# Attention with sinks: the sink as a 129th score column in PSUM, exponentials from PSUM, four probability buffers

## The chip, the cores and the metric

The kernel runs on one core of a Trainium2 chip. The metric is the device time of one execution in microseconds. Before the change three runs gave 2563.44 us (median), 2560.73 us and 2566.36 us.

## The reference

A trunk of two layers over 1024 tokens of width 1024. Each layer has a token mixer and a squared-ReLU MLP, both pre-normalised and modulated. Layer 0 mixes by sliding-window grouped-query attention, the part that the change touches. There are 16 heads of width 64 in two key-value groups of eight; a chunk of 64 queries sees 128 keys (its own chunk and the one before), and each head has a learned sink that takes part in the softmax but has no value:

```python
scores = jnp.einsum('bnqhgd,bnkhd->bnhgqk', q, kk).astype(jnp.float32) * (HEAD_DIM ** -0.5)
scores = jnp.where(valid[None, :, None, None, None, :], scores, -jnp.inf)
m = jnp.maximum(jnp.max(scores, axis=-1, keepdims=True), sink)
p = jnp.exp(scores - m)
probs = p / (jnp.sum(p, axis=-1, keepdims=True) + jnp.exp(sink - m))
o = jnp.einsum('bnhgqk,bnkhd->bnqhgd', probs.astype(vv.dtype), vv)
```

(The last line is the product of the probabilities with the values of the window.) Layer 1 mixes by a chunked gMLP. All is float32.

## The kernel before

Activations lie transposed, features on the partitions and 1024 tokens along the free dimension. The large products run as units of 128 output features: three products of high and low parts (L1034) into the PSUM tile pp[0] or pp[1], with weights loaded by SP, split by ScalarE (L298) and GpSimd (L267).

The attention stage lies between the QKV units and the units of the output projection. It has 32 steps t, two for each of the 16 chunks: t = 2n + g is chunk n and key-value group g. A step works on 4 pairs of heads, r = 0 to 3, each a block of 128 query rows (two heads by 64 queries) by 128 keys. What happens to step t:

- SP loads the queries (`load_q`, L243) into qf[g].
- TensorE `scores` (L1185): four products into one bank of pp[0] (bank g). It waits until the bank is free (p_sub of t - 2) and for the load.
- VectorE `maxima` (L870 to L879): row maxima of the scores, the maximum with 8 times the sink (L872), the sink's column minus the maximum (L877), and the scores minus the maximum from PSUM into the SBUF tile pr[g] (L879). Every small operation waits for the one before by a semaphore.
- ScalarE `exps` (L465): one exponential over 516 columns of pr[g] in place. `window` (L470), every second step, copies the values of the chunk's window.
- VectorE `sums` (L859, L861): row sums and their reciprocals.
- GpSimd `normalise` (L279): pr[g] times the reciprocals.
- TensorE `turn` (L1194): four transposes of pr[g] into a bank of pp[1].
- ScalarE `probs_copy` (L454): that bank into the SBUF tile pt[g].
- TensorE `mix` (L1202): one product with the window's values into a bank of pp[2]; 128 rows are computed, and only the 64 rows of group g are used.
- ScalarE `out_high` (L459) and VectorE `out_low` (L887): the 64 rows by 512 columns as high and low part, once a step.

No planner orders this. Each engine has its own hand-written loop over t, with the steps staggered, and executes it strictly in its order. TensorE in step t does scores(t+1), mix(t-2), turn(t-1). ScalarE does probs_copy(t-2), out_high(t-3), exps(t) and, in even steps, window. VectorE does sums(t-1), maxima(t), out_low(t-3). Four steps make one pass of a hardware loop. After the last step TensorE waits for all `out_low` before the output projection begins (L1034 again), and ScalarE then issues the 8 MB load of mod_late.

Of the kernel before, what the change touches and what calls it, by code (L numbers as in the profile page):

```python
# [48 lines left out]
def build(nc, x_in, c_in, pos_in, weights, mod_w, cols, mats, ws_in, bias_in, q_dram, v_dram, out):  # L49
# [5 lines left out]
    with ctx:  # L55
# [21 lines left out]
        sink8 = sb("sink8", [P, 2 * 4])  # L77
# [8 lines left out]
        with ExitStack() as attn:  # L86
            kf = sb("kf", [HD, KV, PAD + S], f32, attn)
            vt = sb("vt", [P, PAD + S], f32, attn)
            v_s = sb("v_s", [P, NCH, P], f32, attn)
            with ExitStack() as rope:  # L90
                cos = sb("cos", [P, S], f32, rope)
                sin = sb("sin", [P, S], f32, rope)
                qa = sb("qa", [P, 2, S], f32, rope)
                qb = sb("qb", [P, 2, S], f32, rope)
                oa = sb("oa", [P, 2, S], f32, rope)
                ob = sb("ob", [P, 2, S], f32, rope)
            qf = sb("qf", [HD, 2, HALF], f32, attn)
            pr = sb("pr", [P, 2, 4, P + 1], f32, attn)
            pt = sb("pt", [P, 2, HALF], f32, attn)
            v_w = sb("v_w", [P, 2, P], f32, attn)  # L100
            small = sb("small", [P, 2, 4, 4], f32, attn)
# [25 lines left out]
        qgain_a, qgain_b, kgain = (colt[:, o + i:o + i + 1] for i in range(3))  # L127
# [35 lines left out]
        sc_mm, p_sub, p_exp, p_sum, p_norm = sem("sc_mm"), sem("p_sub"), sem("p_exp"), sem("p_sum"), sem("p_norm")  # L163
        p_tr, p_cp, vw, pv_mm, o_hi, o_lo = (sem(n) for n in ("p_tr", "p_cp", "vw", "pv_mm", "o_hi", "o_lo"))
        p_tot, p_max = sem("p_tot"), sem("p_max")
# [9 lines left out]
        sink8_done = sem("sink8_done")  # L175
# [19 lines left out]
        def columns_of(half):  # L195
            return slice(HALF * half, HALF * half + HALF)

# [66 lines left out]
        def _(pool):  # L264
# [12 lines left out]
            def normalise(t, g):  # L277
                pool.wait_ge(p_sum, t + 1)  # L278
                nc.gpsimd.tensor_tensor(out=pr[:, g, :, 0:P], in0=pr[:, g, :, 0:P],  # L279
                                        in1=small[:, g, 3, :].unsqueeze(2).to_broadcast([P, 4, P]),  # L280
                                        op=ALU.mult).then_inc(p_norm, 1)

            with pool.Fori(0, NCH) as n:  # L283
                for g in range(KV):
                    normalise(n * 2 + g, g)
# [7 lines left out]
        def _(act):  # L293
# [156 lines left out]
            def probs_copy(t, g):  # L450
# [3 lines left out]
                nc.scalar.activation(pt[:, g, :], pp[1][:, HALF * g:HALF * g + HALF], ACT.Copy).then_inc(p_cp, 1)  # L454

            def out_high(t, n, g):
                act.wait_ge(pv_mm, t + 1)
                rows = slice(64 * g, 64 * g + 64)
                nc.scalar.activation(h_hi[rows, :, bass.ds(n * CHUNK, CHUNK)],  # L459
                                     pp[2][rows, HALF * g:HALF * g + HALF].rearrange("p (h t) -> p h t", t=CHUNK),  # L460
                                     ACT.Copy).then_inc(o_hi, 1)

            def exps(t, g):
                act.wait_ge(p_sub, t + 1)
                nc.scalar.activation(pr[:, g, :, :], pr[:, g, :, :], ACT.Exp, scale=HD ** -0.5).then_inc(p_exp, 1)  # L465

            def window(t, n, e):
                if not static(t) or t >= 4:
                    act.wait_ge(pv_mm, t - 2)
                nc.scalar.activation(v_w[:, e, :], v_s[:, bass.ds(n, 1), :].rearrange("p a c -> p (a c)"),  # L470
                                     ACT.Copy).then_inc(vw, 1)
# [12 lines left out]

            act.wait_ge(v_cp, 4)
            for b in range(4):
                step(0, b)
            with act.Fori(1, NCH // 2 - 1) as m:
                for b in range(4):
                    step(m, b)  # L490
            for b in range(7):
                step(NCH // 2 - 1 + b // 4, b % 4)
# [11 lines left out]
            act.wait_ge(o_lo, 2 * NCH)  # L504
# [104 lines left out]
        def _(dve):  # L609
# [148 lines left out]
            V.tensor_scalar(sink8[:, :], colt[:, sink0:sink0 + 2 * 4], 8.0, None, ALU.mult).then_inc(sink8_done, 1)  # L758
# [96 lines left out]
            def sums(t, g):  # L855
                dve.wait_ge(p_exp, t + 1)
                if not static(t) or t >= 2:
                    dve.wait_ge(p_norm, t - 1)
                V.tensor_reduce(out=small[:, g, 2, :], in_=pr[:, g, :, :], axis=X, op=ALU.add).then_inc(p_tot, 1)  # L859
                dve.wait_ge(p_tot, t + 1)  # L860
                V.reciprocal(small[:, g, 3, :], small[:, g, 2, :]).then_inc(p_sum, 1)  # L861

            def maxima(t, g):

                lo = PAD if static(t) and t < 2 else 0
                sc = pp[0][:, HALF * g:HALF * g + HALF].rearrange("p (r k) -> p r k", k=P)
                dve.wait_ge(sc_mm, t + 1)
                if not static(t) or t >= 2:
                    dve.wait_ge(p_tr, t - 1)
                V.tensor_reduce(out=small[:, g, 0, :], in_=sc[:, :, lo:], axis=X, op=ALU.max).then_inc(p_max, 1)  # L870
                dve.wait_ge(p_max, t * 2 + 1)
                V.tensor_tensor(out=small[:, g, 1, :], in0=small[:, g, 0, :], in1=sink8[:, 4 * g:4 * g + 4],  # L872
                                op=ALU.max).then_inc(p_max, 1)
                dve.wait_ge(p_max, t * 2 + 2)
                if lo:
                    V.memset(pr[:, g, :, 0:lo], -1.0e4)
                V.tensor_tensor(out=pr[:, g, :, P:P + 1], in0=sink8[:, 4 * g:4 * g + 4].unsqueeze(2),  # L877
                                in1=small[:, g, 1, :].unsqueeze(2), op=ALU.subtract)
                V.tensor_tensor(out=pr[:, g, :, lo:P], in0=sc[:, :, lo:],  # L879
                                in1=small[:, g, 1, :].unsqueeze(2).to_broadcast([P, 4, P - lo]),  # L880
                                op=ALU.subtract).then_inc(p_sub, 1)

            def out_low(t, n, g):
                rows = slice(64 * g, 64 * g + 64)
                cs = bass.ds(n * CHUNK, CHUNK)
                dve.wait_ge(o_hi, t + 1)
                V.tensor_tensor(out=h_lo[rows, :, cs],  # L887
                                in0=pp[2][rows, HALF * g:HALF * g + HALF].rearrange("p (h t) -> p h t", t=CHUNK),
                                in1=h_hi[rows, :, cs].bitcast(f32), op=ALU.subtract).then_inc(o_lo, 1)

            def step(m, b):
                t = m * 4 + b
                if not static(t) or 1 <= t < 2 * NCH + 1:
                    sums(t - 1, (b + 1) % 2)
                if not static(t) or t < 2 * NCH:
                    maxima(t, b % 2)
                if not static(t) or 3 <= t:
                    out_low(t - 3, m * 2 + ((b + 1) // 2 - 2), (b + 1) % 2)

            dve.wait_ge(sink8_done, 1)  # L900
            for b in range(4):
                step(0, b)
            with dve.Fori(1, NCH // 2 - 1) as m:
                for b in range(4):
                    step(m, b)
            for b in range(7):
                step(NCH // 2 - 1 + b // 4, b % 4)
# [112 lines left out]
        def _(pe):  # L1020
# [159 lines left out]
            def scores(t, n, g):  # L1180
                pe.wait_ge(qf_in[g], n * 16 + 16)
                if not static(t) or t >= 2:
                    pe.wait_ge(p_sub, t - 1)
                for r in range(4):
                    last = T.matmul(pp[0][:, HALF * g + P * r:HALF * g + P * r + P], qf[:, g, P * r:P * r + P],  # L1185
# [3 lines left out]
            def turn(t, g):  # L1189
                pe.wait_ge(p_norm, t + 1)  # L1190
                if not static(t) or t >= 2:
                    pe.wait_ge(p_cp, t - 1)
                for r in range(4):
                    last = T.transpose(pp[1][:, HALF * g + P * r:HALF * g + P * r + P], pr[:, g, r, 0:P], ident[:, :])  # L1194
                last.then_inc(p_tr, 1)

            def mix(t, n, g, e):
                pe.wait_ge(p_cp, t + 1)
                pe.wait_ge(vw, n + 1)
                if not static(t) or t >= 2:  # L1200
                    pe.wait_ge(o_lo, t - 1)
                T.matmul(pp[2][:, HALF * g:HALF * g + HALF], v_w[:, e, :], pt[:, g, :],  # L1202
                         start=True, stop=True).then_inc(pv_mm, 1)
# [11 lines left out]
            pe.wait_ge(evac[0], U_WO // 2)  # L1215
# [3 lines left out]
            for b in range(4):  # L1219
                step(0, b)  # L1220
            with pe.Fori(1, NCH // 2 - 1) as m:
                for b in range(4):
                    step(m, b)
            for b in range(6):
                step(NCH // 2 - 1 + b // 4, b % 4)


            pe.wait_ge(o_lo, 2 * NCH)
# [167 lines left out]
```

## Time and profile before

| | us |
|---|---|
| median of the runs | 2563.44 |
| span of the profiled execution | 2568.1 |
| attention stage, first scores to first product of the output projection | 234.07 to 358.36 |

The profiled execution is 4.7 us above the median of the runs. Rows of groups give line, engine, operation, output and inputs with their shapes, the count, the busy time and the mean of one, and the idle time of the engine just before with the engine and line that ended it. Rows in order of time begin with the start and the duration in us; "x8" merges eight instructions, and the bracket holds the idle time before and who ended it. A matmul's end is modelled, so that its duration holds a drain that overlaps with the next; the distance between two starts is what it costs in a queue that doesn't wait. PEclk 1.00 is a granted clock of 2.4 GHz and 0.50 one of 1.2 GHz.

### The profile page before, as it was taken

The numbers are of one execution on the slowest core, as the hardware profiler recorded it, in microseconds if no ns is written. First come the engines' busy times: TensorE is split into PE (matmuls) and PEld (weight loads), VectorE is DVE, ScalarE is ACT, GpSimd is POOL, SyncE is SP. The second block draws the span as 40 slices with busy tenths as digits, with TensorE's granted clock in tenths as the row PEclk, the third lists the DMA queues.
The fourth block names the chain that finished last, engine by engine and source line by source line (L and its number), as shares of the span: only waits on it lengthen the run. The fifth ranks groups of instructions, "written<-read, shape, count | busy, mean of one in ns | idle before, by whom it ended". The sixth has DMA issues, their size and how long they took to land.

```text
span 2568.1 us, 28722 instructions
## 1 busy us (share of the span) xinstructions
PE 2438.0 (95%) x10592; PEld 1942.8 (76%) x10592; DVE 1059.8 (41%) x1190; ACT 650.8 (25%) x719; POOL 506.9 (20%) x232
## 2 busy tenths in 40 slices
PE   3997889899999999998999999999899999999999
PEld 2776458688888888887788788788678888888887
DVE  7655965633333333334432442343522323232232
ACT  3322531321221221212322331122331221221221
POOL 1111221112212212211211112112122221222121
PEclk9887989899999999999999999999899999999999
DMA  6342131121221221221244221221011111111112
GB/s 240 107 140 68 37 150 41 64 84 49 75 80 49 83 72 52 87 66 41 98 127 143 89 74 41 73 82 49 25 49 50 49 41 50 49 47 43 49 49 82
DMA packets 70592, 189.01 MB, mean 74 GB/s; under 512 B 23440, under 2 KB 25360, under 8 KB 70032
## 3 DMA queue, kind: packets, MB, share of 16 engines
q1 hardware_dynamic: 52144, 127.64, 15.4%
q10 hardware_dynamic: 18400, 60.69, 6.8%
q8 instruction: 35, 0.57, 0.1%
q14 instruction: 13, 0.11, 0.0%
HBM read 170.48 MB, written 16.78 MB: 73 GB/s over the span
## 4 chain that ended last, share of the span: by engine, by line
issue 65%; PE 27%; POOL 7%; POOLq 0%; DVE 0%; ACT 0%; DVEq 0%
PE pp L1034 27%; POOL w_lo L267 7%; POOL pr L279 1%; POOLq L287 0%; POOLq L266 0%; DVE x L921 0%; POOLq L283 0%; DVE mod_t L624 0%; ACT tmp L307 0%; POOLq L273 0%; POOLq L278 0%; POOL kf L270 0%; POOLq L267 0%; POOL vt L271 0%; DVEq L921 0%
## 5 line engine op out<-in xcount | busy, mean ns | idle before, releaser
L267 POOL TENSOR_TENSOR w_lo<-w_raw,w_hi 128x1024 fp32r<-128x1024 f32 x194 | 473.2, 2439 | 1942.4 <-ACT w_hi L298 1942.4
L1034 PE MATMUL pp<-h_hi,w_hi 128*128 128x512 f32 x1824 | 605.7, 408 | 35.1 <-DVE h_lo L715 23.3
L1034 PE MATMUL pp<-h_lo,w_hi 128*128 128x512 f32 x1824 | 595.2, 402 | 0.0
L1034 PE MATMUL pp<-h_hi,w_lo 128*128 128x512 f32 x1824 | 593.7, 401 | 0.0
L298 ACT ACTIVATE w_hi<-w_raw 128x1024 fp32r<-128x1024 f32 x194 | 205.0, 1057 | 959.6 <-PE pp L1034 916.9
L1034 PEld LDWEIGHTS pp<-h_hi,w_hi 128*128 128x128 f32 x1824 | 346.6, 192 | 129.3 <-issue 22.4
L1034 PEld LDWEIGHTS pp<-h_lo,w_hi 128*128 128x128 f32 x1824 | 350.5, 192 | 85.3 <-issue 1.0
L1034 PEld LDWEIGHTS pp<-h_hi,w_lo 128*128 128x128 f32 x1824 | 349.6, 192 | 85.7
L1034 PE MATMUL pp<-hid_hi,w_hi 128*128 128x512 f32 x1280 | 410.4, 398 | 0.0
L1034 PE MATMUL pp<-hid_hi,w_lo 128*128 128x512 f32 x1280 | 409.0, 397 | 0.0
L1034 PE MATMUL pp<-hid_lo,w_hi 128*128 128x512 f32 x1280 | 408.9, 397 | 0.0
L921 DVE SCALAR_TENSOR_TENSOR x<-pp,mod,x 128x1024 f32 (+1 forms) x82 | 104.8, 1278 | 481.1 <-PE pp L1034 481.0
L1034 PEld LDWEIGHTS pp<-hid_lo,w_hi 128*128 128x128 f32 x1280 | 241.2, 188 | 59.0 <-issue 0.5
L1034 PEld LDWEIGHTS pp<-hid_hi,w_lo 128*128 128x128 f32 x1280 | 241.2, 188 | 58.7
L1034 PEld LDWEIGHTS pp<-hid_hi,w_hi 128*128 128x128 f32 x1280 | 240.7, 188 | 58.4 <-issue 0.5
L944 DVE SCALAR_TENSOR_TENSOR tmp<-pp,tmp 128x1024 f32<-128x1024 f32 x64 | 78.3, 1224 | 335.2 <-ACT tmp L525 335.2
L624 DVE TENSOR_TENSOR mod_t<-mod_t,tmp 128x1024 f32<-128x1024 f32 x90 | 169.9, 1888 | 105.4 <-ACT tmp L307 104.6
L525 ACT ACTIVATE tmp<-pp 128x1024 f32<-128x1024 f32 x64 | 65.7, 1026 | 472.3 <-PE pp L1034 472.3
L947 DVE TENSOR_TENSOR hid_lo<-tmp,hid_hi 128x1024 f32 x64 | 119.2, 1863 | 87.0 <-ACT hid_hi L528 87.0
L627 DVE SCALAR_TENSOR_TENSOR mod_acc<-mod_t,cond,mod_acc 128x1024 f32<-128x1024 f32 x64 | 95.8, 1497 | 56.2 <-DMA mod_t<-mod_w 55.3
L307 ACT ACTIVATE tmp<-x 128x1024 f32 (+1 forms) x90 | 95.4, 1061 | 81.2 <-DVE x L921 72.8
L974 DVE BATCH_NORM_STATS2 v_stat<-pp 128x128 f32 x128 | 26.9, 282 | 122.6 <-PE pp L1280 122.6
(133 smaller groups left out, 1225.0 us busy)
## 6 DMA issues: line engine op xcount, KB each, us to landing
w_raw<-weights SPq DMA_DIRECT2D x194, 512.0 KB, 3.3
mod_t<-mod_w ACTq DMA_DIRECT2D x64, 512.0 KB, 3.4
mod_first<-mod_w SPq DMA_DIRECT2D x16, 512.0 KB, 15.5
mod_late<-mod_w ACTq DMA_DIRECT2D x2, 4096.0 KB, 19.3
v_dram<-v_out ACTq DMA_DIRECT2D x16, 512.0 KB, 5.5
vf<-v_dram ACTq DMA_DIRECT2D x16, 512.0 KB, 4.4
x<-x_in SPq DMA_DIRECT2D x4, 1024.0 KB, 9.1
qf<-q_dram SPq DMA_DIRECT2D x32, 128.0 KB, 2.5
```

What stands on the lines that cost most here:

```text
L267: nc.gpsimd.tensor_tensor(out=w_lo[:, s, :, :], in0=w_raw[:, s, :, :], in1=w_hi[:, s, :, :].bitcast(f32), op=ALU.subtract).then_inc(lo_don ...
L279: nc.gpsimd.tensor_tensor(out=pr[:, g, :, 0:P], in0=pr[:, g, :, 0:P], in1=small[:, g, 3, :].unsqueeze(2).to_broadcast([P, 4, P]), op=ALU.m ...
L298: nc.scalar.activation(w_hi[:, s, :, :], w_raw[:, s, :, :], ACT.Copy).then_inc(hi_done, 1)
L307: nc.scalar.activation(tmp[:, s, :], x[:, bass.ds(k, 1), :].rearrange("p a s -> p (a s)"), ACT.Square).then_inc(sq_done, 1)
L525: nc.scalar.activation(tmp[:, s, :], pp[s][:, :], ACT.Relu).then_inc(relu, 1)
L624: V.tensor_tensor(out=sumsq, in0=sumsq, in1=tmp[:, s, :], op=ALU.add).then_inc(ss_done, 1)
L627: V.scalar_tensor_tensor(out=mod_acc[:, :], in0=tile, scalar=cond[:, 2, bass.ds(k, 1)], in1=mod_acc[:, :], op0=ALU.mult, op1=ALU.add).then ...
L921: V.scalar_tensor_tensor(out=xn, in0=pp[s][:, :], scalar=mod[:, gate, bass.ds(i * 2 + s, 1)], in1=xn, op0=ALU.mult, op1=ALU.add).then_inc( ...
L944: V.scalar_tensor_tensor(out=tmp[:, s, :], in0=pp[s][:, :], scalar=0.0, in1=tmp[:, s, :], op0=ALU.max, op1=ALU.mult).then_inc(evac[s], 1)
L947: V.tensor_tensor(out=hid_lo[:, bass.ds(i * 2 + s, 1), :].rearrange("p a s -> p (a s)"), in0=tmp[:, s, :], in1=hid_hi[:, bass.ds(i * 2 + s ...
L974: ins = V.bn_stats(v_stat[:, b, bass.ds(c, 1), :].rearrange("p a s -> p (a s)"), pp[2][:, P * b:P * b + P])
L1034: last = T.matmul(pp[s][:, cs], w[:, s, k, :], r[:, k, cs], start=(k == 0 and w is w_hi and r is hi), stop=(k == KC - 1 and w is w_lo))
```

## The change

The attention step is rebuilt:

- The query gain is multiplied by 64 ** -0.5 once (`qgain`), so that scores need no scale, and the sinks are used as they are.
- A score tile is now a whole pp tile (pp[0] for g = 0, pp[3] for g = 1), two banks with 2 x 129 columns each. The sinks are written as column 128 of every block once before the stage and stay there.
- `maxima` is one reduction over 129 columns in PSUM with its result negated. `exps` is four exponentials of 129 columns each that read PSUM, take the negated maximum as bias, and write pr. The maximum with the sink and both subtractions are gone.
- pr and small have four buffers, and `turn` works two steps behind instead of one.
- The two groups' values lie in v_w with zeros between them, so that two `mix` products (g = 0 starts, g = 1 adds) fill all 128 rows of one bank. `out_high` and `out_low` run once per chunk over 128 rows. v_w is zeroed once.
- `probs_copy` is on VectorE for g = 0 and on ScalarE for g = 1.
- The order within a step changes on all three engines: TensorE mix(t-3), scores(t+1), turn(t-2); ScalarE exps(t), window (even t), probs_copy(t-2) (odd t), out_high (even t); VectorE maxima(t), sums(t-1), probs_copy(t-2) (even t), out_low (odd t).
- Scores wait for the exponentials of t - 2 (p_exp), where they waited for the subtraction.

```diff
+        def score_tile(g):
+            return (pp[0], pp[3])[g][:, :].rearrange("p (a c) -> p a c", a=2)[:, :, 0:2 * (P + 1)].rearrange(
+                "p a (b k) -> p a b k", b=2)
...
+            def exps(t, b):
+                lo = PAD if static(t) and t < 2 else 0
+                sc = score_tile(b % 2)
+                act.wait_ge(p_max, t + 1)
+                if not static(t) or t >= 4:
+                    act.wait_ge(p_tr, t - 3)
+                for r in range(4):
+                    ins = nc.scalar.activation(pr[:, b, r, lo:], sc[:, r // 2, r % 2, lo:], ACT.Exp,
+                                               bias=small[:, b, 0, r:r + 1])
+                ins.then_inc(p_exp, 1)
...
             def step(m, b):
                 t = m * 4 + b
-                if not static(t) or 2 <= t < 2 * NCH + 2:
-                    probs_copy(t - 2, b % 2)
-                if not static(t) or 3 <= t:
-                    out_high(t - 3, m * 2 + ((b + 1) // 2 - 2), (b + 1) % 2)
                 if not static(t) or t < 2 * NCH:
-                    exps(t, b % 2)
+                    exps(t, b % 4)
                     if b % 2 == 0:
-                        window(t, m * 2 + b // 2, b // 2)
+                        window(m * 2 + b // 2, (b // 2) % 2)
+                if b % 2 and (not static(t) or 3 <= t < 2 * NCH + 2):
+                    probs_copy(t - 2, m * 2 + ((b - 1) // 2 - 1))
+                if b % 2 == 0 and (not static(t) or t >= 4):
+                    out_high(m * 2 + (b // 2 - 2), (b // 2) % 2)
...
+            def maxima(t, b):
+                lo = PAD if static(t) and t < 2 else 0
+                sc = score_tile(b % 2)
+                dve.wait_ge(sc_mm, t + 1)
+                if lo:
+                    V.memset(pr[:, b, :, 0:lo], 0.0)
+                V.tensor_reduce(out=small[:, b, 0, :].rearrange("p (a b) -> p a b", a=2), in_=sc[:, :, :, lo:], axis=X,
+                                op=ALU.max, negate=True).then_inc(p_max, 1)
+            def probs_copy(t, n):
+                dve.wait_ge(p_tr, t + 1)
                 if not static(t) or t >= 2:
+                    dve.wait_ge(pv_mm, t - 1)
+                V.tensor_copy(pt[:, 0, :], pp[1][:, 0:HALF]).then_inc(p_cp[0], 1)
...
             def step(m, b):
                 t = m * 4 + b
+                if not static(t) or t < 2 * NCH:
+                    maxima(t, b % 4)
                 if not static(t) or 1 <= t < 2 * NCH + 1:
-                    sums(t - 1, (b + 1) % 2)
+                    sums(t - 1, (b + 3) % 4)
+                if b % 2 == 0 and (not static(t) or 2 <= t < 2 * NCH + 2):
+                    probs_copy(t - 2, m * 2 + (b // 2 - 1))
+                if b % 2 and (not static(t) or t >= 5):
+                    out_low(m * 2 + ((b - 1) // 2 - 2), ((b - 1) // 2) % 2)
...
             def step(m, b):
                 t = m * 4 + b
+                if not static(t) or 3 <= t < 2 * NCH + 3:
+                    mix(m * 2 + ((b + 1) // 2 - 2), (b + 1) % 2, ((b + 1) // 2) % 2)
                 if not static(t) or t + 1 < 2 * NCH:
                     scores(t + 1, m * 2 + (b + 1) // 2, (b + 1) % 2)
                 if not static(t) or 2 <= t < 2 * NCH + 2:
-                    mix(t - 2, m * 2 + (b // 2 - 1), b % 2, (b // 2 + 1) % 2)
-                if not static(t) or 1 <= t < 2 * NCH + 1:
-                    turn(t - 1, (b + 1) % 2)
+                    turn(t - 2, m * 2 + (b // 2 - 1), (b + 2) % 4)
```

## Rows read from the trace of the kernel before

**Rows 1.** The page: span, and busy time by engine (share of the span, instructions).
```profile
span 2568.1 us, 28722 instructions
...
PE 2438.0 (95%) x10592; PEld 1942.8 (76%) x10592; DVE 1059.8 (41%) x1190; ACT 650.8 (25%) x719; POOL 506.9 (20%) x232
```

**Rows 2.** Busy time by stretch: bounds, length, then PE, PEld, DVE, ACT, POOL (instructions), PEclk, DMA share, GB/s.
```profile
247.30:305.30 58.00, 47.89 (x235) 28.26 (x235) 54.23 (x115) 30.09 (x58) 16.86 (x17) 1.00 0.13 36
305.30:308.70 3.40, 3.40 (x12) 2.19 (x11) 3.09 (x8) 1.72 (x3) 0.82 (x2) 0.50 0.15 39
...
349.60:363.30 13.70, 10.12 (x22) 5.74 (x21) 4.72 (x8) 3.37 (x6) 1.04 (x1) 0.50 0.30 95
```

**Rows 3.** Groups of instructions, VectorE alone, 253 to 336 us.
```profile
L879 DVE TENSOR_TENSOR pr<-pp,small 128x512 f32<-128x512 f32 x24 | 16.4, 684 | 0.0
L887 DVE TENSOR_TENSOR h_lo<-pp,h_hi 64x512 f32 x24 | 16.4, 683 | 0.4
L870 DVE TENSOR_REDUCE small<-pp 128x4 f32<-128x512 f32 x23 | 15.9, 691 | 0.4
L859 DVE TENSOR_REDUCE small<-pr 128x4 f32<-128x516 f32 x23 | 15.9, 691 | 2.0 <-ACT pr L465 1.0
L872 DVE TENSOR_TENSOR small<-small,sink 128x4 f32<-128x4 f32 x23 | 9.1, 396 | 0.8
L861 DVE RECIPROCAL small<-small 128x4 f32<-128x4 f32 x23 | 4.1, 178 | 0.8
L877 DVE TENSOR_TENSOR pr<-sink,small 128x4 f32<-128x4 f32 x23 | 3.8, 167 | 0.8
```

**Rows 4.** Who waited for whom, 250 to 345 us: total us, times, longest us.
```profile
ACT pr L465 <- DVE pr L879: 46.3, 27, 1.9
...
PE pp L1185 <- DVE pr L879: 5.6, 24, 0.3
```

**Rows 5.** Groups of instructions, ScalarE and GpSimd, 236 to 358 us.
```profile
L279 POOL TENSOR_TENSOR pr<-pr,small 128x512 f32<-128x512 f32 x32 | 33.3, 1039 | 94.9 <-DVE small L861 94.9
...
L465 ACT ACTIVATE pr<-pr 128x516 f32<-128x516 f32 x32 | 20.3, 633 | 54.8 <-DVE pr L879 54.8
L454 ACT ACTIVATE pt<-pp 128x512 f32<-128x512 f32 x32 | 18.8, 588 | 3.5 <-PE pp L1194 3.1
...
L470 ACT ACTIVATE v_w<-v_s 128x128 f32 (+1 forms) x16 | 4.7, 293 | 0.0
```

**Rows 6.** TensorE in order of time, first steps of the stage.
```profile
239.09 2.07 PE L1185 MATMUL pp<-kf,qf 64*128 64x128 f32 x8 [1.24 <-DMA qf<-q_dram]
...
244.79 2.07 PE L1202 MATMUL pp<-pt,v_w 128*128 128x512 f32 x2
...
248.57 1.13 PE L1202 MATMUL pp<-pt,v_w 128*128 128x512 f32 x2
249.53 0.60 PE L1194 MATMUL pp<-ident,pr 128*128 128x128 f32 x4
250.06 1.16 PE L1185 MATMUL pp<-kf,qf 64*128 x8
251.15 1.12 PE L1202 MATMUL pp<-pt,v_w 128*128 128x512 f32 x2
...
253.29 1.15 PE L1185 MATMUL pp<-kf,qf 64*128 x8 [0.18 <-DVE pr L879]
```

**Rows 7.** TensorE in order of time, last scores to the output projection.
```profile
342.90 1.13 PE L1185 MATMUL pp<-kf,qf 64*128 64x128 f32 x8 [0.25 <-DVE pr L879]
...
352.95 1.06 PE L1194 MATMUL pp<-ident,pr 128*128 128x128 f32 x4
...
354.70 2.07 PE L1202 MATMUL pp<-pt,v_w 128*128 128x512 f32 x2 [0.69 <-ACT pt L454]
...
358.36 1.19 PE L1034 MATMUL pp<-h_hi,w_hi 128*128 128x512 f32 x2 [1.59 <-DVE h_lo L887]
```

More of the change, by code:

```diff
@@ L76, in build @@
         inv = sb("inv", [P, 4 * KC])
-        sink8 = sb("sink8", [P, 2 * 4])
+        qgain = sb("qgain", [P, 2])
         with ExitStack() as first:
@@ L126, in build @@
         o = 4 * KC + PARTS * KC
-        qgain_a, qgain_b, kgain = (colt[:, o + i:o + i + 1] for i in range(3))
+        kgain = colt[:, o + 2:o + 3]
+        qgain_a, qgain_b = qgain[:, 0:1], qgain[:, 1:2]
         inv_freq = colt[:, o + 3:o + 4]
@@ L275, in _, with normalise @@
                     split_lo(pair, s)
-            def normalise(t, g):
+            def normalise(t, b):
                 pool.wait_ge(p_sum, t + 1)
-                nc.gpsimd.tensor_tensor(out=pr[:, g, :, 0:P], in0=pr[:, g, :, 0:P],
-                                        in1=small[:, g, 3, :].unsqueeze(2).to_broadcast([P, 4, P]),
+                nc.gpsimd.tensor_tensor(out=pr[:, b, :, 0:P], in0=pr[:, b, :, 0:P],
+                                        in1=small[:, b, 3, :].unsqueeze(2).to_broadcast([P, 4, P]),
                                         op=ALU.mult).then_inc(p_norm, 1)
-            with pool.Fori(0, NCH) as n:
-                for g in range(KV):
-                    normalise(n * 2 + g, g)
+            with pool.Fori(0, NCH // 2) as m:
+                for b in range(4):
+                    normalise(m * 4 + b, b)
             with pool.Fori(U_WO // 2 + 1, UNITS // 2) as pair:
@@ L453, in probs_copy, with out_high, window @@
                     act.wait_ge(pv_mm, t - 1)
[L454 to L460, printed above, removed]
-                                     ACT.Copy).then_inc(o_hi, 1)
[L463 to L470, printed above, removed]
+                nc.scalar.activation(pt[:, 1, :], pp[1][:, HALF:], ACT.Copy).then_inc(p_cp[1], 1)
+            def out_high(n, e):
+                act.wait_ge(pv_mm, n * 2 + 2)
+                nc.scalar.activation(h_hi[:, :, bass.ds(n * CHUNK, CHUNK)],
+                                     pp[2][:, HALF * e:HALF * e + HALF].rearrange("p (h t) -> p h t", t=CHUNK),
+                                     ACT.Copy).then_inc(o_hi, 1)
+            def window(n, e):
+                if not static(n) or n >= 2:
+                    act.wait_ge(pv_mm, n * 2 - 2)
+                nc.scalar.activation(v_w[:, e, :].rearrange("p (g c) -> p g c", g=2)[:, :, 0:HD],
+                                     v_s[:, bass.ds(n, 1), :].rearrange("p a (g c) -> p (a g) c", g=KV),
                                      ACT.Copy).then_inc(vw, 1)
@@ L475, in step @@
                 t = m * 4 + b
[L476 to L479 removed]
                 if not static(t) or t < 2 * NCH:
[L481 removed]
+                    exps(t, b % 4)
                     if b % 2 == 0:
[L483 to L488 removed]
+                        window(m * 2 + b // 2, (b // 2) % 2)
[3 more added lines that the diff above has]
+                    out_high(m * 2 + (b // 2 - 2), (b // 2) % 2)
+            act.wait_ge(v_cp, 4)
+            act.wait_ge(vw_zero, 1)
+            for m in range(2):
+                for b in range(4):
+                    step(m, b)
+            with act.Fori(2, NCH // 2 - 1) as m:
                 for b in range(4):
@@ L491, in _ @@
             for b in range(7):
-                step(NCH // 2 - 1 + b // 4, b % 4)
+                step(NCH // 2 - 1, b)
             def residual(pair0, first=0, count=4, split=True):
@@ L757, in _ @@
             dve.wait_ge(const_in, 48)
-            V.tensor_scalar(sink8[:, :], colt[:, sink0:sink0 + 2 * 4], 8.0, None, ALU.mult).then_inc(sink8_done, 1)
+            own(V.tensor_scalar(qgain[:, :], colt[:, o:o + 2], HD ** -0.5, None, ALU.mult))
             dve.wait_ge(pos_s, 16)
@@ L852, in _, with sums @@
             mod_part(3)
-            def sums(t, g):
+            def sums(t, b):
                 dve.wait_ge(p_exp, t + 1)
-                if not static(t) or t >= 2:
[L858 to L881, printed above, removed]
@@ L883, in out_low @@
-            def out_low(t, n, g):
-                rows = slice(64 * g, 64 * g + 64)
+                if not static(t) or t >= 4:
+                    dve.wait_ge(p_norm, t - 3)
+                V.tensor_reduce(out=small[:, b, 2, :], in_=pr[:, b, :, :], axis=X, op=ALU.add).then_inc(p_tot, 1)
+                dve.wait_ge(p_tot, t + 1)
+                V.reciprocal(small[:, b, 3, :], small[:, b, 2, :]).then_inc(p_sum, 1)
+            def maxima(t, b):
[6 more added lines that the diff above has]
+                                op=ALU.max, negate=True).then_inc(p_max, 1)
@@ L885, in out_low, with probs_copy @@
+            def probs_copy(t, n):
+                dve.wait_ge(p_tr, t + 1)
+                if not static(t) or t >= 2:
+                    dve.wait_ge(pv_mm, t - 1)
+                V.tensor_copy(pt[:, 0, :], pp[1][:, 0:HALF]).then_inc(p_cp[0], 1)
+            def out_low(n, e):
                 cs = bass.ds(n * CHUNK, CHUNK)
[L886 to L889, printed above, removed]
+                dve.wait_ge(o_hi, n + 1)
+                V.tensor_tensor(out=h_lo[:, :, cs],
+                                in0=pp[2][:, HALF * e:HALF * e + HALF].rearrange("p (h t) -> p h t", t=CHUNK),
+                                in1=h_hi[:, :, cs].bitcast(f32), op=ALU.subtract).then_inc(o_lo, 1)
@@ L901, in _ @@
-            for b in range(4):
-                step(0, b)
-            with dve.Fori(1, NCH // 2 - 1) as m:
+                    sums(t - 1, (b + 3) % 4)
[3 more added lines that the diff above has]
+                    out_low(m * 2 + ((b - 1) // 2 - 2), ((b - 1) // 2) % 2)
+            dve.wait_ge(evac[0], U_WO // 2)
+            dve.wait_ge(v_cp, 4)
@@ L904, in _ @@
+            for g in range(KV):
+                V.tensor_copy(score_tile(g)[:, :, :, P:P + 1],
+                              colt[:, sink0 + 4 * g:sink0 + 4 * g + 4].rearrange("p (a b k) -> p a b k", a=2, b=2)).then_inc(sinks_in, 1)
+            dve.wait_ge(sinks_in, 2)
+            dve.wait_ge(q_out, 16 * 8 * 4)
+            dve.wait_ge(kf_in, 16 * 4)
+            V.memset(v_w[:, :, :], 0.0).then_inc(vw_zero, 1)
+            for m in range(2):
                 for b in range(4):
                     step(m, b)
-            for b in range(7):
-                step(NCH // 2 - 1 + b // 4, b % 4)
+            with dve.Fori(2, NCH // 2 - 1) as m:
+                for b in range(4):
+                    step(m, b)
@@ L910, in residual @@
+            for b in range(8):
+                step(NCH // 2 - 1, b)
             def residual(pair0, n0, gate, first=0, count=4, late=None, zeroed=None):
@@ L1218, in _ @@
             scores(0, 0, 0)
-            for b in range(4):
-                step(0, b)
-            with pe.Fori(1, NCH // 2 - 1) as m:
+            for m in range(2):
                 for b in range(4):
                     step(m, b)
-            for b in range(6):
-                step(NCH // 2 - 1 + b // 4, b % 4)
-            pe.wait_ge(o_lo, 2 * NCH)
+            with pe.Fori(2, NCH // 2 - 1) as m:
+                for b in range(4):
+                    step(m, b)
+            for b in range(7):
+                step(NCH // 2 - 1, b)
+            pe.wait_ge(o_lo, NCH)
             for late in range(2):
```

53 lines of the change are left out of this document (25 added, 28 removed).

## The prediction

> **What bounds the kernel now.** I read the page's busy times first: TensorE is busy for 95% of the span and VectorE for 41% [rows 1]. That average says nothing of the attention stage, so I went on to the windows. In the first 58 us of full clock in that stage VectorE is busy for 54.23 of 58.00 us, TensorE for 47.89, ScalarE for 30.09 and GpSimd for 16.86 [rows 2]. One step takes 3.584 us: the scores of step 6 start at 253.29 [rows 6] and those of step 31 at 342.90 [rows 7], 89.61 us for 25 steps. The groups of VectorE add up to 0.684 + 0.683 + 0.691 + 0.691 + 0.396 + 0.178 + 0.167 = 3.490 us a step [rows 3], with almost no idle time. So VectorE sets the pace, and the waits say the same: ScalarE's exponential waited for the subtraction in each of 27 steps, and TensorE's scores in 24 [rows 4]. TensorE follows closely. Where it ran from a queue that didn't wait (248.57 to 251.15), mix took 0.96 us from start to start, turn 0.53 and scores 1.09, or 2.58 us in all [rows 6].
>
> **What VectorE loses.** Per pair of steps the new code has two maxima and two sums (4 x 0.691), two reciprocals (2 x 0.178), one out_low (0.684; it covers 128 rows, with the same 512 columns) and one copy out of PSUM. No row shows such a copy on VectorE: ScalarE's takes 0.588 [rows 5], and VectorE's operations of that width out of PSUM take 0.684 to 0.691 [rows 3]. I take 0.691, the same engine. The pair comes to 4.495 us, or 2.25 us a step instead of 3.49. If VectorE or the queued TensorE (2.58) still set the pace, the stage would shrink by about 1.0 us a step.
>
> **What the new order makes of TensorE.** This step decides. Before, the order was turn(t-1), then scores(t+2), then mix(t-1): the copy of the transposed probabilities ran under the scores. Now a step is mix(t-3), scores(t+1), turn(t-2), and the next begins with mix(t-2), which waits for the copy of exactly what turn(t-2) has just written. Nothing of TensorE's lies between. Step by step:
> - mix start to scores start: 0.96 (mix to turn) [rows 6];
> - scores start to turn start: 1.09 (scores to mix) [rows 6];
> - turn from start to end: 0.60 [rows 6];
> - end of turn, semaphore, copy on ScalarE, semaphore, start of mix: 0.69, seen whole in the tail, where nothing else was in the way [rows 7].
>
> This makes 3.34 us for an odd step, whose copy is on ScalarE. An even step has VectorE's copy, 0.10 us longer (0.691 against 0.588), so 3.44. The mean is 3.39 us. TensorE is then a serial chain with one hole of about 0.7 us per step, and VectorE idles a third of the time.
>
> The copier must be free when turn ends, 2.65 us into the step. VectorE: after an odd step's out_low it takes maxima (when the scores end, some 2.2 us into the step), and sums, and reaches the copy about 0.4 us into the even step: free. Maxima(t+1) is queued behind the copy and so starts at 3.4 us; the exponential of that odd step starts 0.7 us into it, and ScalarE has until 2.65 for it, a slack of 1.95 us. Price of the four exponentials: a 128-column activation takes 0.293, so 4 x 0.293 = 1.17; were the fixed part free, it would be the 0.633 of 516 columns [rows 5]. I take 1.17 (the row with the same width): it fits either way and costs nothing. If that cover is gone, every microsecond above 1.95 is paid in every second step.
>
> The Trainium skill speaks against this edit: ScalarE: Activation LUTs, "Rules for kernel authors", budgets about 0.3 us for each activation plus 0.83 ns an element, four times over 1.63 us. By that page the step would still fit, with 0.3 us of slack instead of 0.8; the trace's 0.293 us for 128 columns is less than the rule's 0.41.
>
> The rest hides. Normalise stays at 1.039 us on GpSimd [rows 5] and, with four buffers, has a step more before its turn needs it. The scores' wait for exponentials of t - 2 is met over a step earlier. Out_high falls to once in two steps; ScalarE's load for a pair is 2 x 1.17 + 0.588 + 0.588 + 0.293 = 3.8 of 6.8 us. SP's query loads keep their place. Zeroing v_w (768 columns, at most 1.0 us by the rate of 512 columns in 0.691) and writing the sinks are queued ahead of the first maxima, while the first key load and scores are under way; the qgain operation replaces sink8 early.
>
> **The sum.** Against the profiled execution (span 2568.1):
> - Start. The third scores now wait for the first exponentials and begin at about 239.3 (239.09 before). Then at low clock two scores (2.07 each, as before), turn (1.06), copy (0.69), mix (2.07), and from the clock's rise scores 1.09, turn 0.60, copy 0.69: mix(1) at 249.6 [rows 6, 7]. Scores of step 6 follow mix(2): 249.6 + 3.39 + 0.96 = 254.0, where 253.29 stood: +0.7.
> - 25 steps at 3.39 instead of 3.584: -4.85.
> - Tail. From the last scores to the projection it took 358.36 - 342.90 = 15.46 us [rows 7]. Now, from those scores: turn(28) ends at 1.69, mix(28) at 2.48; without scores the following steps are mix 0.96, turn 0.60, copy 0.69 or 0.79, so mix(29) at 4.73, mix(30) at 7.08, mix(31) at 9.33; the mix itself takes 1.12 and the two output copies took 1.59 (358.36 less 354.70 + 2.07): 12.04 us, a gain of 3.42. The last exponentials and their normalising end near 6.7, before turn(31) at 8.04. That is at full clock. Before, the clock fell to 1.2 GHz at 349.6 and stayed there for 13.7 us [rows 2], and if it does so again from mix(30), two mixes and a turn lengthen by 0.95 + 0.46 + 0.95 = 2.4 and the gain is 1.1.
>
> Sum: 0.7 - 4.85 - 3.42 = -7.6 with a warm tail, 0.7 - 4.85 - 1.1 = -5.2 with a cold one. Should the projection also start warm, half of the 4.9 us from 358.36 to 363.3 comes on top: -10.1. TensorE pauses in the tail as often as before but more briefly, so I take the middle of the first two, -6.4. The later stages depend on nothing in this one except its end: the mod_late load and the projection start together, as before. The median of the runs is 4.7 us below the profiled execution's span, and I move it by the same amount: 2563.4 - 6.4 = 2557.0.
>
> **The rivals.**
> - Exponentials from PSUM slower than thought, or copies caught behind other work on ScalarE or VectorE. Each 0.4 us more on the hole costs 0.4 x 29 = 12 us. An exponential stage of 2.2 us (0.55 each) would add 0.25 in every second step, +4: 2561. For it: four instructions with a bias operand from PSUM, which no row shows. Against it: 0.8 us of slack. The page named above would sharpen it without reaching it. Chance 0.10, mostly "same".
> - The slower side: the granted clock. The hole is now one piece of 0.7 us every step, and the clock already dropped once in mid-stage, at 305.30, for 3.4 us, though TensorE was busy around it [rows 2]. Before, low clock in mid-stage was covered, since VectorE set the pace. Now every TensorE term lies in the chain: a low step costs 2.07 + 2.07 + 1.06 + 0.7 = 5.9 less overlaps of some 0.2, 5.7 instead of 3.39, or +2.3. It decides from 5 low steps on (6.4 + 5.1 = 11.5 us, 28 us of low clock). If it stayed low for 20 of the 31, 2557.0 + 46 = 2603. Against it: TensorE's work in a step is the same as before and the step is shorter, so its share of work rises from 2.58 / 3.584 to 2.58 / 3.39. Chance 0.09.
> - The serial chain doesn't hold, because the rows' modelled ends overstate it: if the chain is only the queued 2.58 plus 0.4, 3.0 us a step, this gives 29 x 0.4 = 12 us more: 2545. The wait for the copy is in the program's order, so I give it 0.06.
> - The chain as summed: 0.75.
>
> **How the numbers follow.** A measurement of this kernel can tell about 0.2%, 5.1 us, from no change. The forecast's own cases run from -3 (start worse, cold tail) to -10, and the cold tail stands right at that bound: of its 0.75 I put 0.54 beyond and 0.21 within. The first rival gives 0.08 to same and 0.02 to slower, the clock 0.09 to slower, the last 0.06 to faster. Faster 0.60, same 0.29, slower 0.11. The range reaches from 2550 (warm throughout, with part of the last rival) to 2565 (copies late by 0.25 in every step, +7).
>
> **What would show it.** In the profile after: step period 3.3 to 3.5 us; TensorE's mix waits about 0.7 us in nearly every step for the copy, half of the time on ScalarE and half on VectorE; VectorE idles about 1.1 us a step, most of it before its copy, ended by the transposes; four exponentials take 0.8 to 1.2 us together; the projection starts 5 to 8 us earlier. It is wrong if mix waits much longer than 0.8 us, if the scores wait for exponentials, or if PEclk shows 0.50 in the stage for more than one short piece.

## The result, and the profile after

The changed kernel takes 2631.36 us (median of 4 runs, 2627.88 to 2635.11) against 2564.67 us for the kernel before (median of 4, a run of 2565.90 us having joined the three of the first section): a ratio of 1.0261 with a 95% interval of 1.0244 to 1.0277. It is slower by 67 us where 6 us less were forecast.

The page of the changed kernel comes first: span, busy times, and TensorE's granted clock in 40 slices.

```profile
span 2627.4 us, 28569 instructions
...
PE 2494.2 (95%) x10592; PEld 1973.4 (75%) x10592; DVE 1023.1 (39%) x1097; ACT 649.9 (25%) x783; POOL 506.5 (19%) x232
...
PEclk8996557999999999999899999999899999999999
```

VectorE has lost 37 us of work against [rows 1], as intended. TensorE has 56 us more, with the same number of products: they have become slower. PEclk shows where, in the slices from about 200 to 420 us. The window of the stage (columns as in [rows 2]):

```profile
240.00:400.00 160.00, 139.38 (x380) 81.08 (x380) 56.97 (x110) 49.35 (x152) 29.15 (x28) 0.50 0.08 21
```

The granted clock is 0.50, or 1.2 GHz, for the whole 160 us; the kernel before had 1.00 over most of the stage [rows 2]. TensorE in order of time shows how the stage begins, a step, and how it ends:

```profile
228.96 3.78 PE L1210 MATMUL pp<-kf,qf 64*128 64x128 f32 x16 [3.17 <-DMA kf<-oa]
...
253.48 2.07 PE L1210 MATMUL pp<-kf,qf 64*128 64x128 f32 x8
...
257.29 2.07 PE L1229 MATMUL pp<-pt,v_w 128*128 128x512 f32 x2 [0.69 <-ACT pt L474]
259.29 2.07 PE L1210 MATMUL pp<-kf,qf 64*128 64x128 f32 x8
261.30 1.11 PE L1220 MATMUL pp<-ident,pr 128*128 128x128 f32 x4
263.19 2.08 PE L1229 MATMUL pp<-pt,v_w 128*128 128x512 f32 x2 [0.78 <-DVE pt L896]
...
400.64 2.07 PE L1210 MATMUL pp<-kf,qf 64*128 64x128 f32 x8
...
415.49 2.07 PE L1229 MATMUL pp<-pt,v_w 128*128 128x512 f32 x2 [0.69 <-ACT pt L474]
419.15 1.19 PE L1059 MATMUL pp<-h_hi,w_hi 128*128 128x512 f32 x2 [1.59 <-DVE h_lo L901]
```

Mix (L1229), scores (L1210), turn (L1220), then a hole of 0.69 us where ScalarE copies and 0.78 us where VectorE does. That is the serial chain of the forecast, with each term at the low clock: 2.00 + 2.01 + 1.11 + 0.78 = 5.90 us for the step from 257.29 to 263.19, and 5.81 us where the hole is 0.69. From the scores of step 6 (253.48) to those of step 31 (400.64) it is 147.16 us for 25 steps, 5.89 us each instead of 3.584. From 240 to 400 us the engine waits for nothing else:

```profile
PE pp L1229 <- DVE pt L896: 11.8, 14, 0.9
PE pp L1229 <- ACT pt L474: 9.6, 14, 0.7
```

The first scores stood at 228.96 and the projection began at 419.15: 190.2 us for the stage, where the table gave 124.3. These 66 us are the result; what follows the stage takes 2208.3 us (2627.4 less 419.15) against 2209.7. What precedes it took 5.1 us less than in the profile of the kernel before (228.96 against 234.07), but this part scatters: in the profiles of the experiments below whose code is the same up to there, the first scores stand anywhere from 228.99 to 236.20. The length of the stage is therefore the better measure of one profile against another.

### The profile page after: what moved, and what is told of

The parts are those of the page before. It is cut to its first block, busy times and chain, and to the rows that moved or that the text cites. A ratio compares the mean times of both kernels' runs of the same rounds, so it can differ in the third digit from the quotient of the medians.

```text
span 2627.4 us, 28569 instructions
## 1 busy us (share of the span) xinstructions
PE 2494.2 (95%) x10592; PEld 1973.4 (75%) x10592; DVE 1023.1 (39%) x1097; ACT 649.9 (25%) x783; POOL 506.5 (19%) x232
## 4 chain that ended last, share of the span: by engine, by line
issue 65%; PE 27%; POOL 8%; POOLq 0%; DVE 0%; ACT 0%; DVEq 0%
PE pp L1059 27%; POOL w_lo L274 7%; POOL pr L286 1%; POOLq L294 0%; POOLq L273 0%; DVE x L946 0%; DVE mod_t L642 0%; ACT tmp L314 0%; POOLq L285 0%; POOLq L290 0%; POOLq L280 0%; POOL kf L277 0%; POOLq L274 0%; POOL vt L278 0%; DVEq L946 0%
## 5 line engine op out<-in xcount | busy, mean ns | idle before, releaser
L1210 PEld LDWEIGHTS pp<-kf,qf 64*128 64x128 f32 x256 | 56.8, 325 | 47.0 <-issue 42.1
```

Source lines behind the costliest of these rows:

```text
L1210: last = T.matmul(score_tile(g)[:, r // 2, r % 2, 0:P], qf[:, g, P * r:P * r + P], kf[:, g, bass.ds(n * CHUNK, P)], start=True, stop=True)
```

## The experiments

Two theories were set against each other. By the first, the new order of TensorE's step makes a hole in each step, and with it a clock that starts low never rises. By the second, something else of the change (the score tiles of two banks, exponentials from PSUM, too little work in a step) slows the stage, and the order doesn't matter.

### Scores ahead of mix again

```diff
             def step(m, b):
                 t = m * 4 + b
-                if not static(t) or 3 <= t < 2 * NCH + 3:
-                    mix(...)
                 if not static(t) or t + 1 < 2 * NCH:
                     scores(...)
+                if not static(t) or 3 <= t < 2 * NCH + 3:
+                    mix(...)
```

> The changed kernel with one edit: in TensorE's step scores(t+1) stands before mix(t-3) again, so that it covers the copy between turn and mix. Theory 1 (the order makes a hole in every step, and the granted clock stays at 1.2 GHz as long as it is there): no hole, the clock rises to 2.4 GHz within the first steps, a step takes 2.6 to 2.8 us instead of 5.86, the stage shrinks from about 189 us to about 100, total 2530 to 2545 us. Theory 2 (the clock stays low because each step has too little work for TensorE, whatever the order): a clock of 1.2 GHz throughout, steps of about 5.1 us (2.00 + 2.00 + 1.1), total about 2607 us.

Measured: 2538.98 us (2535.81 to 2541.32), ratio to the kernel before 0.991 (0.9888 to 0.9932). Swapping two calls is worth 92 us against the changed kernel. TensorE in order of time, and the window of the loop:

```profile
248.64 1.21 PE L1210 MATMUL pp<-kf,qf 64*128 64x128 f32 x8
249.79 1.12 PE L1229 MATMUL pp<-pt,v_w 128*128 128x512 f32 x2
250.75 0.60 PE L1220 MATMUL pp<-ident,pr 128*128 128x128 f32 x4
251.37 1.13 PE L1210 MATMUL pp<-kf,qf 64*128 64x128 f32 x8
...
316.05 1.13 PE L1210 MATMUL pp<-kf,qf 64*128 64x128 f32 x8
```
```profile
253.00:315.00 62.00, 60.00 (x324) 40.56 (x323) 46.72 (x91) 41.41 (x125) 23.82 (x23) 1.00 0.16 49
```

The hole ahead of mix is gone, the clock is 1.00, and TensorE is busy for 60 of 62 us. From the scores of step 6 (248.64) to those of step 31 (316.05) it is 67.41 us for 25 steps, 2.70 us each. So the new arithmetic does what it is for; VectorE, busy for 46.72 of 62 us, no longer sets the pace.

### The hole in the kernel before

The converse, with none of the new arithmetic:

```diff
             def step(m, b):
                 t = m * 4 + b
+                if not static(t) or 2 <= t < 2 * NCH + 2:
+                    mix(t - 2, ...)
                 if not static(t) or t + 1 < 2 * NCH:
                     scores(t + 1, ...)
-                if not static(t) or 2 <= t < 2 * NCH + 2:
-                    mix(t - 2, ...)
                 if not static(t) or 1 <= t < 2 * NCH + 1:
                     turn(t - 1, (b + 1) % 2)
```

> The kernel before with one edit: mix(t-2) stands ahead of scores(t+1) in TensorE's step, so that it follows turn(t-2) directly. Nothing of the new arithmetic. Theory 1: the same hole, the clock stays low through the stage, steps of about 5.8 us instead of 3.58, total 2620 to 2640 us. Theory 2 (something else of the change, such as the score tiles of two banks or exponentials from PSUM, holds TensorE down): the clock is high as before, VectorE sets the pace, total 2560 to 2575 us.

Measured: 2629.4 us, ratio 1.0261 (1.0234 to 1.0289), the very ratio of the whole change. A step takes 5.86 us. A window of its stage, and some of its steps:

```profile
260.00:400.00 140.00, 122.56 (x336) 71.47 (x335) 74.46 (x168) 44.08 (x84) 24.93 (x24) 0.50 0.07 22
```
```profile
247.83 2.07 PE L1202 MATMUL pp<-pt,v_w 128*128 128x512 f32 x2 [0.69 <-ACT pt L454]
249.83 2.07 PE L1185 MATMUL pp<-kf,qf 64*128 64x128 f32 x8
251.84 1.11 PE L1194 MATMUL pp<-ident,pr 128*128 128x128 f32 x4
253.90 2.07 PE L1202 MATMUL pp<-pt,v_w 128*128 128x512 f32 x2 [0.95 <-ACT pt L454]
```

The second theory falls with these two runs: the order alone makes the loss, and taking the order away removes the loss.

### Filling the hole with work that nobody needs

```diff
+            def fill(g, count):
+                for i in range(count):
+                    T.matmul(pp[1][:, HALF * (1 - g):HALF * (1 - g) + P], ident[:, :], ident[:, :], start=True, stop=True)
...
                     turn(t - 2, m * 2 + (b // 2 - 1), (b + 2) % 4)
+                    fill(b % 2, 2)
```

> The changed kernel, order untouched, with two extra 128x128x128 float32 products after each turn, into the bank of pp[1] that is free then; nothing reads them. They fill TensorE's hole with work that helps nobody. Theory 1 (the hole holds the clock down): the clock rises, a step takes 3.4 to 3.6 us, total 2555 to 2570 us although TensorE does more. Theory 2 (the order or the copies are slow for another reason, and the clock only follows): steps of 5.9 us as before the edit or more, total 2630 to 2640 us.

Measured: 2562.88 us (2557.54 to 2565.47), ratio 0.9996 (0.9985 to 1.0007). With the order of the changed kernel, and more work for TensorE, 68 us come back. In the profile the clock rose at about 253 us, and a step then took 3.57 us, as it does with open holes at high clock (the run with the filled start below). It is the clock, then, that makes the hole dear, not the hole's own 0.7 us.

> As filled (the changed kernel with extra products after each turn), but with one product instead of two, so that at low clock about 0.43 us of the 0.7 to 0.78 us hole are filled and 0.3 remain in every step. If any pause in every step holds the clock down: steps of 5.86 us, total 2625 to 2635 us. If it depends on the pause's share: the clock rises, steps of 3.5 us, total 2560 to 2568 us. I hold the second for likelier, since the kernel before rose from low clock with small pauses between its groups.

This one has `fill(b % 2, 1)`. Measured: 2565.54 us (2561.08 to 2572.82), ratio 1.0006 (0.9992 to 1.002). At low clock 0.36 us of hole were left ahead of the first mix, and the next group already ran fast:

```profile
244.05 0.63 PE L1234 MATMUL pp<-ident 128*128 128x128 f32 x2
245.04 2.08 PE L1229 MATMUL pp<-pt,v_w 128*128 128x512 f32 x2 [0.36 <-DVE pt L896]
247.05 1.16 PE L1210 MATMUL pp<-kf,qf 64*128 64x128 f32 x8
```

The time is that of the second branch, and one pause of 0.36 us didn't keep the clock from rising. The first branch isn't excluded by it: only that one short pause stood at low clock, the ones after it (0.46 to 0.72 us) came at high clock, so a short pause in every step at low clock remains untested.

### Filling at the start only

The same edit under `if static(t) and t < 8`: the extra products stand in the eight unrolled steps, and the loop is that of the changed kernel.

> As filled, but the extra products stand only in the first eight steps, which are unrolled; the loop over the other steps is that of the changed kernel. Theory 1a (low clock holds itself: once it is high, the steps of 3.4 us with 0.7 us of hole keep it high, since TensorE's share of work is larger than in the kernel before): clock 2.4 GHz to the tail, total about 2560 us. Theory 1b (the hole also pulls a high clock down): the clock falls again after the filled steps, steps of 5.86 us, total 2610 to 2630 us.

Measured: 2561.94 us (2557.96 to 2566.85), ratio 0.9996 (0.9984 to 1.0008). In the loop, long after the last extra product:

```profile
271.42 1.12 PE L1229 MATMUL pp<-pt,v_w 128*128 128x512 f32 x2 [0.94 <-DVE pt L896]
272.47 1.16 PE L1210 MATMUL pp<-kf,qf 64*128 x8
273.56 0.66 PE L1220 MATMUL pp<-ident,pr 128*128 128x128 f32 x4
274.91 1.13 PE L1229 MATMUL pp<-pt,v_w 128*128 128x512 f32 x2 [0.69 <-ACT pt L474]
...
278.49 1.12 PE L1229 MATMUL pp<-pt,v_w 128*128 128x512 f32 x2 [0.78 <-DVE pt L896]
...
285.71 1.12 PE L1229 MATMUL pp<-pt,v_w 128*128 128x512 f32 x2 [0.95 <-DVE pt L896]
...
347.26 1.16 PE L1210 MATMUL pp<-kf,qf 64*128 64x128 f32 x8
...
359.37 0.70 PE L1059 MATMUL pp<-h_hi,w_hi 128*128 128x512 f32 x2 [1.59 <-DVE h_lo L901]
```
```profile
270.00:333.00 63.00, 48.96 (x244) 29.13 (x243) 37.88 (x72) 31.42 (x97) 18.26 (x18) 1.00 0.12 38
```

The same instructions in the same order, with the same holes, keep a clock of 1.00 for the whole loop (and here to the end of the stage). The four steps from 271.42 to 285.71 take 14.29 us, 3.57 us each. The loop has two states, and the start chooses. Theory 1a holds and 1b falls.

> The kernel before with mix ahead of scores, and two extra products after each turn in its first eight steps only, as in filled_start. None of the new arithmetic. Theory 1a (two states of the same loop: low clock and a chain of 5.8 us, or high clock; what the start gives, stays): the clock is high after the start, and a step takes the longer of VectorE's 3.5 us and the chain's 3.4, so 3.5 to 3.6: total 2562 to 2572 us. Theory 1b (this loop falls back to low clock because VectorE's work adds pauses): 2610 to 2630 us.

This is the same test on the kernel before with its hole (eight steps unrolled on TensorE). Measured: 2565.24 us (2561.14 to 2570.07), ratio 1.0007 (0.9993 to 1.0021), against 2629.4 us without the filled start. Its window:

```profile
260.00:345.00 85.00, 66.58 (x339) 40.61 (x340) 79.64 (x168) 44.50 (x84) 23.94 (x24) 1.00 0.12 34
```

Again two states of one loop, at a clock of 0.50 or of 1.00. From the scores of step 8 to those of step 31 a step took 3.73 us, a little more than the 3.5 to 3.6 expected.

### A burst ahead of the stage

```diff
+            pe.wait_ge(evac[1], U_WO // 2)
+            fill(0, 7)
             pe.wait_ge(kf_in, 16 * 4)
             pe.wait_ge(sinks_in, 2)
-            pe.wait_ge(evac[1], U_WO // 2)
             pe.wait_ge(q_cs, 8)
             scores(0, 0, 0)
```

> The changed kernel, its steps untouched, with seven extra 128x128x128 float32 products ahead of the first scores, while TensorE waits for the keys (about 3 us at low clock). Theory 1 (a step with the hole never raises a low clock; only what comes before the stage or fills the steps can): the pauses of the first steps undo the burst, or it raises the clock in time. If it raises it and the hole doesn't pull it down again (as in the run with filled first steps), total about 2555 us. If the first four scores and the pause of 1.4 us for the first exponentials come at low clock still, it stays low: total 2625 to 2635 us. I hold the second for likelier (0.6), since one burst with a pause behind it is less than the eight filled steps.

Measured: 2626.79 us, ratio 1.0245 (1.0212 to 1.0278). The total is what the second branch gave, but the way is different: the burst did raise the clock, and it fell again. TensorE in order of time, then three windows:

```profile
229.98 3.33 PE L1243 MATMUL pp<-ident 128*128 128x128 f32 x14
233.25 2.44 PE L1210 MATMUL pp<-kf,qf 64*128 64x128 f32 x16
237.94 3.75 PE L1210 MATMUL pp<-kf,qf 64*128 64x128 f32 x16 [2.25 <-ACT pr L465]
```
```profile
233.80:237.00 3.20, 1.89 (x16) 1.69 (x14) 1.49 (x5) 1.42 (x2) 0.00 (x0) 0.95 0.13 44
237.00:240.40 3.40, 2.46 (x11) 2.49 (x12) 1.25 (x3) 1.82 (x9) 1.04 (x1) 0.57 0.14 39
240.40:400.00 159.60, 138.91 (x383) 81.45 (x382) 57.57 (x111) 49.03 (x152) 29.13 (x28) 0.50 0.08 23
```

The products of the first two scores ran in 2.44 us instead of 3.78; then TensorE waited 2.25 us for the first exponentials, the clock fell, and it stayed at 0.50. The fall came in front of the first mix, so no hole of a step had a part in it; that it stayed low in the steps behind is what the changed kernel does too.

> The kernel with scores ahead of mix, with the same burst of seven products ahead of the first scores and three more after the second ones, where TensorE waits for the first exponentials. The clock rose there at 248 us, 19 us after the first scores. Theory 1 (pauses ahead of and in the first steps delay the rise): it rises by 238 us, and some 10 us at low clock turn into 5: total 2533 to 2536 us. Rival (the rise depends on the steps alone): no change, 2537 to 2541 us.

This adds, beside the burst, three products after the second scores, to the kernel with scores ahead of mix. Measured: 2530.95 us (2530.24 to 2532.94), ratio 0.987 (0.9846 to 0.9894), the fastest of all, and below the range expected. The third and fourth scores here and in the kernel without the burst (the first row is of the one with it):

```profile
234.89 2.15 PE L1210 MATMUL pp<-kf,qf 64*128 64x128 f32 x16 [1.39 <-ACT pr L465]
```
```profile
234.20 3.75 PE L1210 MATMUL pp<-kf,qf 64*128 64x128 f32 x16 [1.44 <-ACT pr L465]
```

A pause of 1.39 us in place of 2.25 us left the clock high. The medians are 8 us apart, taken on two chips. The profiles tell of 6.3 us in the stage: 93.76 us from the first scores (230.17) to the projection (323.93), against 100.04 (228.99 to 329.03) without the burst. That is what the burst, with the rise before 235 us instead of at 248, is worth; the other 2 us aren't explained.

### The hole in every second step

Scores stand ahead of mix where b is even, behind it where b is odd.

> The changed kernel with scores ahead of mix in even steps only, so that at low clock TensorE works without a pause for two steps less one hole (about 10 us) and then waits 0.78 us for VectorE's copy. If a stretch without a pause is what lets the clock rise: it rises in the first steps, and at 2.4 GHz the steps take 2.6 and 3.6 us in turn: total 2545 to 2555 us. If a hole anywhere in the loop holds it down: steps of 5.1 and 5.9 us, total 2610 to 2620 us.

Measured: 2550.15 us (2547.86 to 2552.01), ratio 0.9944 (0.9922 to 0.9967).

```profile
241.56 2.08 PE L1229 MATMUL pp<-pt,v_w 128*128 128x512 f32 x2 [0.78 <-DVE pt L896]
...
248.62 2.07 PE L1229 MATMUL pp<-pt,v_w 128*128 128x512 f32 x2
...
252.33 1.12 PE L1229 MATMUL pp<-pt,v_w 128*128 128x512 f32 x2 [0.78 <-DVE pt L896]
...
281.10 1.12 PE L1229 MATMUL pp<-pt,v_w 128*128 128x512 f32 x2
...
283.44 1.12 PE L1229 MATMUL pp<-pt,v_w 128*128 128x512 f32 x2 [0.78 <-DVE pt L896]
...
287.25 1.12 PE L1229 MATMUL pp<-pt,v_w 128*128 128x512 f32 x2
```

One hole stood at low clock (ahead of 241.56), then 10 us without a pause; behind the second hole the clock was high. In the loop, mix waits in every second step only. The starts of mix are 2.34 us apart where no scores stand between them (281.10 to 283.44) and 3.81 us where two do (283.44 to 287.25): 6.15 us for two steps, between twice 2.70 and twice 3.57. With the hole in every second step the clock rose; with it in each step it did not.

## Why the prediction was wrong

- **What bounds the kernel: right.** VectorE's work fell as reckoned: the copy out of PSUM took 0.69 us, as taken, and two subtractions and the sink's maximum are gone. With scores ahead of mix the stage became bound by TensorE at 2.70 us a step, near the 2.58 of [rows 6].
- **The serial chain: right in its structure.** Mix waits for the copy in every step, 0.69 us for ScalarE and 0.78 us for VectorE, as in the sum. At high clock, in the run with the filled start, the chain takes 3.49 us for the step from 271.42 to 274.91 and 3.58 for the next (to 278.49); over a whole pass of four steps the mean is 3.57 instead of 3.39. The error of 0.18 lies in three terms: mix to scores took 1.05, where 0.96 was taken from mix to turn; a turn that follows scores lasts 0.66, not 0.60; and at the start of each pass of the loop the hole is 0.94 or 0.95 us instead of 0.78, 0.04 a step.
- **The tail: right at high clock.** From the last scores to the projection it was 12.11 us in that run (359.37 less 347.26), 12.04 in the sum. The low clock of the tail that the kernel before had didn't come there.
- **The exponentials: right in their sum, partly by luck.** Four of them stood in 1.14 to 1.15 us, where 1.17 was taken and where the rule of the Trainium skill (ScalarE: Activation LUTs, "Rules for kernel authors") gives an estimate of 1.63. But the 0.293 behind the 1.17 is the row of a plain copy of 128 columns. One exponential takes 0.369 us, and only because the four overlap in the trace do they need less than four times that. They never held up a copy. The row from the loop with scores ahead of mix, 253 to 315 us:

```profile
L465 ACT ACTIVATE pr<-pp,small 128x129 f32<-128x129 f32 x90 | 25.9, 369 | 16.3 <-DVE small L888 16.3
```

- **The step that failed** is the first term of the sum: "at low clock two scores, turn, copy, mix, and from the clock's rise scores 1.09". The rise at 247 us was carried over from the kernel before, as if it came at a time of its own. In the kernel before, TensorE had run without a pause for 5.5 us when the clock rose (the scores at 247.48 are the first fast group):

```profile
241.75 1.11 PE L1194 MATMUL pp<-ident,pr 128*128 128x128 f32 x4 [0.59 <-POOL pr L279]
...
247.48 1.16 PE L1185 MATMUL pp<-kf,qf 64*128 64x128 f32 x8
```

In the changed order every step at low clock has its hole, and the rise never came within the stage. The 25 steps at 3.39 and the tail fell with it, since they were summed at the high clock. From the first scores to those of step 6, for the 25 steps, and from the last scores to the projection, the sum had 19.9 + 84.8 + 12.0 = 116.7 us (119.1 with the cold tail); the profile has 24.5 + 147.2 + 18.5 = 190.2. The forecast's own sign of being wrong, PEclk at 0.50 in the stage for more than one short piece, is what was seen.
- **The rival on the granted clock** named the mechanism and its price (+2.3 us a step, which is 5.89 less 3.57 as measured; 5.7 us a step forecast), but had 0.09 of the chance and a wrong reason against it: that TensorE's share of work rises from 2.58 / 3.584 to 2.58 / 3.39. That compares two loops that are already at high clock. The state in which the stage begins is the low one, and there the question is whether it is ever left. By the record's busy time TensorE was even busier in the slow loop (139.38 of 160 us, 87%) than in the fast one with the same code (48.96 of 63 us, 78%), since its products take longer there; a share read at one clock can't be set against a share read at the other. The rival's own case stopped at 20 steps and 2603 us. With the start, all 25 steps and the tail as measured (24.5 against 19.9; 5.89 against 3.39; 18.5 against 13.2, the middle of the two cases), it would have been 2557.0 + 4.6 + 62.4 + 5.3 = 2629, near the measured 2631.

Of the 67 us, then: the new arithmetic and the four buffers bring about -24 us when the order covers the copy (2538.98 against 2562.84). The order costs 23 us of that at high clock (2561.94 with the filled start), and the clock that it holds down another 69 (2631.36 against 2561.94). The lengths of the stage in the profiles say the same: 124.3 us before, 100.0 with the copy covered, 123.2 with the filled start and 190.2 as changed, so -24.3, +23.1 and +67.0; some 3 us more come behind the stage, where the projection began at high clock after the filled start (2205.3 us from there to the end, against 2208.3).

That it is the holes in each step at low clock is shown by removing, filling and moving them, in both kernels. Whether a hole shorter than 0.69 us in each step would still let the clock rise isn't known: with one extra product the clock was high after a single hole of 0.36 us.

## What to carry to other kernels

In an in-order engine's step, put independent work between an operation and the one that waits for its copy; counting the work of each engine doesn't show that such cover is gone. Where a stage begins at TensorE's low clock, sum its steps at that clock first and look for a pause in each of them: a clock rise seen in the kernel before may not be carried over. A few products that nobody reads, put into the first steps, showed here at once that the stage was slow by its clock and not by its work.

## What the runs showed that was not expected

The same loop, instruction for instruction, ran at 5.89 us a step or at 3.57 us, by its first steps alone, and kept either state to its end (160 us of clock 0.50, or 63 us and more of 1.00). A raised clock was lost to one pause of 2.25 us and survived one of 1.39 us. Products that nobody reads, ahead of a stage that needs no more cover, took 6 us off the stage and 8 us off the median (2538.98 to 2530.95).

How long TensorE works without a pause doesn't settle by itself when the clock rises. In the kernel before with the hole and the filled start it rose within 3.6 us of the last pause (0.64 us, ahead of 238.74), in the kernel before after 5.5 us, with scores ahead of mix after 14 us (234.20 to 248.6). In the changed kernel 28 stretches of 5.1 us between holes brought no rise. The runs show that the hole in each step decides here; what exactly is decisive in it stays open.
